# One block of four in the modulation sums: a product with columns of ones in place of a transpose, in a two-block transformer kernel

## What is computed

```python
def ada_modulation(c, ada_w, ada_b):
    m = jax.nn.silu(c) @ ada_w + ada_b
    return jnp.split(m, N_MOD, axis=-1)
```

## Time and profile before

| what | value |
|---|---|
| median of 3 runs | 1195.1 us (1194.32 to 1201.52) |
| the profiled execution, its own time | 1198.31 us |
| its span in the profile | 1196.7 us |
| PE busy | 1181.8 us, 99% |
| DVE busy | 865.3 us, 72% |
| ACT busy | 636.4 us, 53% |
| DMA | 250.00 MB, mean 209 GB/s |

### The profile page before, as it was taken

How to read it: one execution, slowest core, us unless ns; L and a number is a source line. 1 busy time by engine, 2 the same in 40 slices (tenths; PEclk the granted TensorE clock), 3 DMA queues, 4 the chain that set the end, 5 groups by cost and what they waited for, 6 DMA issues and landing times.

```text
span 1196.7 us, 23369 instructions
## 1 busy us (share of the span) xinstructions
PE 1181.8 (99%) x9635; PEld 1146.2 (96%) x9635; DVE 865.3 (72%) x1148; ACT 636.4 (53%) x854; POOL 95.6 (8%) x147
## 2 busy tenths in 40 slices
PE   8999999999999999999999999999999999999998
PEld 8999999999998999999999999999988779999998
DVE  5776888778786788777889988886476557845443
ACT  7557566624337567634368463443455665543332
POOL 0000011110115011111100001110000000000000
PEclk9999999999999999999999999999999999999999
DMA  9452588887772488778754557876645505565352
GB/s 335 160 171 77 176 289 273 287 289 259 272 259 77 150 279 307 256 289 302 268 199 142 179 173 255 284 264 226 218 160 184 168 1 174 179 210 164 125 192 82
DMA packets 150298, 250.00 MB, mean 209 GB/s; under 512 B 5537, under 2 KB 80906, under 8 KB 150218
## 3 DMA queue, kind: packets, MB, share of 16 engines
q1 hardware_dynamic: 136098, 198.21, 49.4%
q0 software_dynamic: 13952, 50.60, 11.7%
q10 hardware_dynamic: 168, 0.04, 0.0%
HBM read 247.79 MB, written 1.05 MB: 208 GB/s over the span
## 4 chain that ended last, share of the span: by engine, by line
PE 92%; DVE 5%; ACT 1%; issue 1%; ACTq 0%; POOL 0%; DVEq 0%
PE ps L2155 27%; PE ps L2157 27%; PE ps L2156 27%; DVE w_lo L1257 2%; PE ps L2423 2%; PE ps L2293 1%; PE ps L2734 1%; PE ps L2405 1%; PE ps L2209 1%; PE ps L2708 1%; PE ps L2392 1%; PE ps L2748 1%; PE ps L2236 0%; PE ps L2391 0%; ACT h_both L808 0%
## 5 line engine op out<-in xcount | busy, mean ns | idle before, releaser
L1257 DVE TENSOR_TENSOR w_lo<-raw,w_hi 128x2048 fp32r<-128x2048 f32 (+4 forms) x196 | 412.7, 2144 | 102.0 <-ACT w_hi L741 101.7
L741 ACT ACTIVATE w_hi<-raw 128x2048 fp32r<-128x2048 f32 (+4 forms) x196 | 342.0, 1790 | 168.2 <-PE ps L2157 168.2
L2155 PE MATMUL ps<-h_both,w_hi 128*128 128x256 f32 (+1 forms) x1296 | 363.5, 280 | 3.1 <-issue 1.1
L2157 PE MATMUL ps<-h_both,w_lo 128*128 128x256 f32 (+1 forms) x1296 | 361.1, 279 | 0.0
L2156 PE MATMUL ps<-h_both,w_hi 128*128 128x256 f32 (+1 forms) x1296 | 361.1, 279 | 0.0
L2155 PEld LDWEIGHTS ps<-h_both,w_hi 128*128 128x128 f32 (+1 forms) x1296 | 242.7, 187 | 4.6 <-issue 2.8
L2156 PEld LDWEIGHTS ps<-h_both,w_hi 128*128 128x128 f32 (+1 forms) x1296 | 245.0, 189 | 0.1
L2157 PEld LDWEIGHTS ps<-h_both,w_lo 128*128 128x128 f32 (+1 forms) x1296 | 243.1, 188 | 0.0
L2155 PE MATMUL ps<-a_both,w_hi 128*128 128x256 f32 x864 | 241.7, 280 | 0.0
L2156 PE MATMUL ps<-a_both,w_hi 128*128 128x256 f32 x864 | 240.8, 279 | 0.0
L2157 PE MATMUL ps<-a_both,w_lo 128*128 128x256 f32 x864 | 240.8, 279 | 0.0
(11 more groups left out here) (422 smaller groups left out, 1823.5 us busy)
## 6 DMA issues: line engine op xcount, KB each, us to landing
ada_raw<-in_l_ada_w POOLq DMA_DIRECT2D x96, 512.0 KB, 6.5
raw<-in_mlp_w_up SPq DMA_DIRECT2D x32, 1024.0 KB, 6.6
raw<-in_mlp_w_down SPq DMA_DIRECT2D x32, 1024.0 KB, 7.0
raw<-in_l_ffn_w_gate SPq DMA_DIRECT2D x22, 1024.0 KB, 5.5
raw<-in_l_ffn_w_up SPq DMA_DIRECT2D x22, 1024.0 KB, 8.0
raw<-in_l_ffn_w_down SPq DMA_DIRECT2D x16, 768.0 KB, 5.7
raw<-in_l_w_qkv SPq DMA_DIRECT2D x12, 1024.0 KB, 6.7
raw<-in_l_w_in SPq DMA_DIRECT2D x10, 1024.0 KB, 6.5
```

Source lines behind the costliest of these rows:

```text
L741: nc.scalar.activation(w_hi[:, s.slot, cut], raw[:, s.slot, cut], ACT.Copy).then_inc(split_hi, 1)
L1257: nc.vector.tensor_tensor(w_lo[:, s.slot, cut], raw[:, s.slot, cut], w_hi[:, s.slot, cut].bitcast(F32), ALU.subtract).then_inc(split_lo, 1)
L2155: nc.tensor.matmul(to, sh, mh, start=first, stop=False, skip_group_check=True)
L2157: return nc.tensor.matmul(to, sl, mh, start=False, stop=last, skip_group_check=True)
```

## The change

Of the four blocks of a group, three are transposed as before, and DVE sums them along rows, now 128x384 to 128x3. The fourth block is the stationary operand of a product with two columns of ones: the result is the sum over its partitions, as a column, twice side by side. DVE copies one of the two into `ada_cols` by an instruction of its own. The product is float32, like the transposes; its output goes to the two first columns of the quarter that the fourth transpose filled.

```diff
+ADA_TURNED = 3
...
-                ins = nc.vector.tensor_reduce(to, ps[:, ADA_BANK, :].rearrange("p (q k) -> p q k", q=4), AX.X, ALU.add)
+                nc.vector.tensor_reduce(to[:, 0:ADA_TURNED], ps[:, ADA_BANK, 0:ADA_TURNED * P].rearrange("p (q k) -> p q k", q=ADA_TURNED), AX.X, ALU.add)
+                ins = nc.vector.tensor_copy(to[:, ADA_TURNED:4], ps[:, ADA_BANK, ADA_TURNED * P::P])
...
                 for q in range(4):
-                    ins = nc.tensor.transpose(ps[:, ADA_BANK, q * P:(q + 1) * P],
-                                              scratch[:, 2 + q // 2, (q % 2) * P:(q % 2 + 1) * P], ident[:, :])
+                    block = scratch[:, 2 + q // 2, (q % 2) * P:(q % 2 + 1) * P]
+                    if q < ADA_TURNED:
+                        ins = nc.tensor.transpose(ps[:, ADA_BANK, q * P:(q + 1) * P], block, ident[:, :])
+                    else:
+                        ins = nc.tensor.matmul(ps[:, ADA_BANK, q * P:q * P + 2], block, ones[:, 0:2], start=True, stop=True, skip_group_check=True)
                 ins.then_inc(ada_reduced, 1)
```

## The result

The changed kernel takes 1208.16 us (median of 20 runs, 1203.0 to 1213.07), the kernel before 1196.43 us in the same comparison; the ratio is 1.009, with a 95% interval of 1.0075 to 1.0105. Forecast were +2.3 us; it is slower by about 11. The profiled execution has a span of 1207.8 us against 1196.7.

The account below looks back on a forecast made before the run. PE was taken as the bound, fed throughout. A pair of loads in place of one transpose adds 0.11 us in 21 groups, +2.3 us, with DVE at nothing: 1195.1 becomes 1197.4 us, range 1193.5 to 1201.0.

Parts of the forecast that it names:

- Which rows bound the kernel: Whole kernel: PE is fed throughout, so work added to its queue moves the end, unless PE waits right behind it.
- A pair of loads, 0.22 us, +0.11 a group: Each group: the two-column product is two block loads, 0.22 us, replacing a 0.11 us transpose, so +0.11 us.
- Loads that hide: Rival at the new product: its loads slip beside neighbouring products, 21 x -0.11 = -2.3 us, 1192.8 us; chance 0.09.
- four loads: Rival at the new product: four block loads, +0.33 us a group, +6.9 us, 1202.0 us; 0.08 together with the 256-column price.
- the 256-column price: Rival: two columns cost what 256 do, 0.43 us, so a group loses 0.32 us; 0.08 together with four loads.
- DVE at nothing: DVE's shorter reduction plus copy: +0.02 us a group, +1.2 to +4.5 us in all, costed at nothing behind its waits.
- Three groups swallow the addition: At the first, tenth and eleventh groups, PE waits or a slow product just behind absorb the added 0.11 us.
- The other 21 run straight into products. Sum on PE: 21 x 0.11: The remaining groups have no PE wait behind them and each pay 0.11 us, +2.3 us in all.
- The clock as the only way to slower by over 1%: Rival: PE's clock halves in products behind each group, from 2.4 to 1.2 GHz, giving 1219 to about 1311 us; chance 0.02.
- The Trainium skill's four passes: At the new product: true float32 takes four array passes, perhaps two per record; read literally, four loads.
- A gain of over 1% has no mechanism: taking out all the transposes would give 10.6 us: All 24 groups' transposes total 10.6 us, under the 12 us of 1%; faster by over 1% given 0.01.
- The range: Whole-kernel time 1193.5 to 1201.0 us, leaving out about 2 in 10, with the median's own uncertainty put at 2 us either side.

Follow-up runs that it names:

- wide_product: The changed kernel with 128 columns of ones streamed in the product instead of two; 1210.45 us, ratio 1.0109 to the kernel before.
- dve_only: The kernel before with its four transposes on PE, but the change's shorter reduction and column copy on DVE; 1199.55 us, ratio 1.0007.
- again_before: The kernel before, with no edit, run and profiled once more; 1198.29 us, ratio 1.000.
- product_third: The changed kernel with each group's order made transpose, transpose, product, transpose, same work; 1187.57 us, ratio 0.9932 to the kernel before.
- tail_four_three: The kernel before with five transposes a group, plus four and then three more behind two slots of the last gate and up projections; 1189.16 us, one run.
- five: The kernel before with five transposes a group, the fourth block's twice, DVE as before; 1193.31 us, ratio 0.9951.
- five_again: Five transposes a group once more, against the kernel before, with no other edit; 1189.33 us, ratio 0.9965.

## Why the prediction was wrong

- *Which rows bound the kernel*: right in the main. PE is fed in both, and the end moved with PE's queue, but for the places behind the first and the eleventh group, where a PE that comes earlier waits longer.
- *A pair of loads, 0.22 us, +0.11 a group*: right, 0.79 for 0.68. wide_product, with 64 times the columns at the same price, bears out that two columns cost what more do, up to 128. Loads that hide, four loads, the 256-column price: none of them happened; the records are x48.
- *DVE at nothing*: right, by dve_only; +0.02 us a read was 0.550 + 0.147 - 0.684 = +0.013.
- *Three groups swallow the addition*: right for the first. Behind the tenth and the eleventh the waits grew instead of shrinking, +1.3 us together. Neither is a cost of the group. The one behind the eleventh goes with the fast stretch ahead of it, as said above; the one ahead of the scores is 0.38 and 1.3 us in two traces of the same kernel (before and again_before), and what sets it wasn't tested.
- *"The other 21 run straight into products. Sum on PE: 21 x 0.11"*: this is the step that failed. It takes the products around a group as fixed, at "0.115" each. There are two steps, 0.1133 and 0.1178, and what stands between stretches sets which. That was about 7.7 of the 11.1 us. The 0.115 is from the earlier trace rows, where 0.11 and 0.12 stand side by side. That is rounding within the first products of one slow stretch (0.115, 0.118 and 0.117 us in the trace), so these rows couldn't show it: the fast stretch ends just ahead of them. A count of records in two windows would have shown it.
- *The clock as the only way to slower by over 1%*: the right place to look, the products behind the group, with the wrong cause. The granted clock reads 1.00 in fast and slow windows alike.
- *The Trainium skill's four passes* ("FP8 and Floating Point Precision", section "TensorE Precision Notes") as four loads: the trace has two records, two loads. Its other reading, two passes within a record, is left standing and was not tested.
- *"A gain of over 1% has no mechanism: taking out all the transposes would give 10.6 us"*: the bound doesn't hold, though no run here gained over 1%. product_third is 8 us faster than before with nothing taken out of PE's queue: its groups cost 0.06 us more each. The gain is in products outside the group, which the bound left out.
- *The range*: the two heaps of the runs of before were treated as noise of 2 us. As far as the traces show, they were the mark of the effect, 6 us for one stretch.

What stays open is why. Shown are the two steps, that they hold for a stretch, and that the order within the group turns the result. What each kind of group does is counted here where the product follows at once, over the traces in which it stands:

| group | stretches behind it |
|---|---|
| four transposes | 63 of 70 have the other step than the one ahead |
| six transposes | 21 of 21 have the other step |
| five transposes | 110 of 110 fast, two of them behind a slow one |
| three transposes | 20 of 20 fast, none of them behind a slow one; that case was seen once, in tail_four_three |
| three transposes, then the product | 19 of 20 slow (20 of 21 with 128 columns) |
| two transposes, the product, a transpose | 20 of 20 fast |

The seven exceptions of the four transposes and the two of the products all stand at the first group of a PE loop (L2470 or L2634); there four transposes changed the step in 5 of 12 cases, everywhere else in 58 of 58. Not shown is what in the engine differs, and what entering a loop has to do with it. No theory of mine forecast product_third; the nearest of the three outcomes written down for it was 1190 to 1192.

## What to carry to other kernels

Where PE is the bound, measure the step of the main product in several stretches, by counting its records in windows of equal length, before pricing a change at its own line: 4% of the step over 1260 products, 5.7 us, was more than the 2.5 us of the edit itself. If stretches of the same product differ at the same clock, try the small work between them in other orders and in odd and even numbers, since that costs nothing and was worth about 20 us here between two orders of the same five records (1208.16 and 1187.57 us). Runs in two heaps are worth explaining before a comparison is made on them.

## What the hardware showed that I had not expected

- A float32r product of 256 columns in a steady stream takes 0.1133 or 0.1178 us at a granted clock of 1.00, for up to 1260 products without a change.
- One transpose more in each of 24 groups, 2.6 us of added queue at 0.11, made the kernel 0.35 to 0.5% faster (five, five_again).
- A float32 product of two columns costs two block loads, 0.22 us as the last of a group, and with 128 columns the same. Ahead of a transpose it costs less, 0.74 in place of 0.79 us for the group (product_third).
